# Latent attention of a decoder layer: values in token order, keys in a bank of their own, splits moved, probability turns behind the gate product

## The reference

```python
q = (rms_norm(c_q, q_norm) @ w_uq).reshape(b, s, MLA_HEADS, QK_NOPE + QK_ROPE)      # 384 -> 8 heads x (64 + 32)
kv = (rms_norm(c_kv, kv_norm) @ w_ukv).reshape(b, s, MLA_HEADS, QK_NOPE + V_DIM)    # 256 -> 8 heads x (64 + 64)
k_nope, v = kv[..., :QK_NOPE], kv[..., QK_NOPE:]
# the 32 rotated key features are shared by the heads
logits = q_full @ k_full * (QK_NOPE + QK_ROPE) ** -0.5, causal
y_a = softmax(logits) @ v @ w_br_mla
```

## Time and profile before

| what | value |
|---|---|
| median of 3 runs | 1281.73 us (1281.72 to 1281.84) |
| the profiled execution | 1280.79 us |
| its span | 1279.0 us |
| TensorE busy | 1267.3 us, 5998 matrix instructions |
| Vector, Scalar, GpSimd busy | 669.7, 441.7, 18.8 us |
| granted TensorE clock | 0.998 of full speed |
| latent section on the trace | from 407.0 to 536.9 us |

### The profile page before, as it was taken

The page is one execution under the profiler, slowest core; times in us unless marked ns, Lnnn a source line. Parts: engine busy times, 40 slices in busy tenths (PEclk is TensorE's granted clock), DMA queues, the critical chain, the costliest instruction groups (busy, mean ns, idle before and its releaser), DMA issues.

```text
span 1279.0 us, 16611 instructions
## 1 busy us (share of the span) xinstructions
PE 1267.3 (99%) x5998; PEld 1033.5 (81%) x5998; DVE 669.7 (52%) x984; ACT 441.7 (35%) x763; POOL 18.8 (1%) x36
## 2 busy tenths in 40 slices
PE   9999999999999999999999999999999999999997
PEld 6888888888888777788888888888888888888886
DVE  6744444433336677475665746675644444443323
ACT  6233332322233444343343424423433332232221
POOL 0000000000000000300000000000000000000000
PEclk9999999999999999999999999999999999999999
DMA  6342223333322221622222231222322322233321
GB/s 214 101 111 98 98 98 98 90 91 95 103 92 71 64 70 66 132 67 83 79 78 92 66 99 51 97 89 95 99 96 98 98 98 98 98 90 92 93 88 66
DMA packets 36003, 118.38 MB, mean 93 GB/s; under 512 B 4680, under 2 KB 4680, under 8 KB 35968
## 3 DMA queue, kind: packets, MB, share of 16 engines
q1 hardware_dynamic: 34416, 114.83, 27.8%
q0 software_dynamic: 1264, 3.06, 1.5%
q10 hardware_dynamic: 288, 0.03, 0.0%
HBM read 115.36 MB, written 2.55 MB: 92 GB/s over the span
## 4 chain that ended last, share of the span: by engine, by line
PE 94%; DVE 2%; DMA 1%; issue 1%; ACT 1%; SPq 0%; DVEq 0%; ACTq 0%
PE bank L542 36%; PE bank L376 17%; PE bank L378 17%; PE bank L377 17%; PE bank L725 1%; PE bank L751 1%; PE bank L645 1%; PE bank L672 1%; DVE mla_stats L1451 1%; DMA x<-in_x_t 1%; PE bank L661 1%; PE bank L769 1%; PE bank L765 1%; DMA const<-in_tables 0%; ACT w_hi L358 0%
## 5 line engine op out<-in xcount | busy, mean ns | idle before, releaser
L363 DVE TENSOR_TENSOR w_lo<-raw,w_hi 128x1024 fp32r<-128x1024 f32 (+2 forms) x221 | 258.8, 1171 | 227.6 <-ACT w_hi L358 225.4
L358 ACT ACTIVATE w_hi<-raw 128x1024 fp32r<-128x1024 f32 (+2 forms) x221 | 224.3, 1015 | 433.3 <-PE bank L542 228.3
L542 PE MATMUL bank<-act_hi,w_hi 128*128 128x512 f32 x704 | 218.5, 392 | 0.3 <-DVE w_lo L363 0.3
L542 PE MATMUL bank<-act_hi,w_lo 128*128 128x512 f32 x704 | 217.0, 389 | 0.0
L542 PE MATMUL bank<-act_lo,w_hi 128*128 128x512 f32 x704 | 216.9, 389 | 0.0
L376 PE MATMUL bank<-act_hi,w_hi 128*128 128x512 f32 x528 | 210.7, 399 | 2.0 <-DVE w_lo L363 1.2
L378 PE MATMUL bank<-act_hi,w_lo 128*128 128x512 f32 x528 | 206.2, 390 | 0.0
L377 PE MATMUL bank<-act_lo,w_hi 128*128 128x512 f32 x528 | 205.9, 390 | 0.0
L542 PEld LDWEIGHTS bank<-act_hi,w_hi 128*128 128x128 f32 x704 | 132.2, 188 | 29.6 <-DVE w_lo L363 1.0
L542 PEld LDWEIGHTS bank<-act_hi,w_lo 128*128 128x128 f32 x704 | 132.2, 188 | 27.5
L542 PEld LDWEIGHTS bank<-act_lo,w_hi 128*128 128x128 f32 x704 | 132.2, 188 | 27.4
(11 more groups left out here) (177 smaller groups left out, 1049.3 us busy)
## 6 DMA issues: line engine op xcount, KB each, us to landing
raw<-in_ffn_up SPq DMA_DIRECT2D x87, 512.0 KB, 3.3
raw<-in_w_dil SPq DMA_DIRECT2D x40, 512.0 KB, 3.3
raw<-in_ffn_down SPq DMA_DIRECT2D x32, 448.0 KB, 3.3
raw<-in_ffn_down SPq DMA_DIRECT2D x16, 512.0 KB, 3.5
raw<-in_w_mla_gates SPq DMA_DIRECT2D x8, 512.0 KB, 3.3
raw<-in_w_branches SPq DMA_DIRECT2D x8, 512.0 KB, 3.3
raw<-in_w_out SPq DMA_DIRECT2D x8, 512.0 KB, 3.2
raw<-in_w_latent SPq DMA_DIRECT2D x6, 512.0 KB, 3.3
```

Source lines behind the costliest of these rows:

```text
L358: nc.scalar.activation(w_hi[:, s % SPLIT, 0:tiles * P], raw[:, s % RAW, 0:tiles * P], ACT.Copy).then_inc(hi_ready, 1)
L363: nc.vector.tensor_tensor(w_lo[:, s % SPLIT, 0:tiles * P], raw[:, s % RAW, 0:tiles * P], w_hi[:, s % SPLIT, 0:tiles * P].bitcast(F32), ALU ...
L542: last = nc.tensor.matmul(out, w[:, s % SPLIT, tile * P:(tile + 1) * P], moving[:, row, :], start=row == 0 and w is w_hi and moving is act_hi,
```

## The change

Values: one new group of products (`values`) at the head of the section computes the values of all 8 heads with tokens as rows, from a new piece of weights (`w_values`, 8 tiles): for each block of 128 tokens and each of two latent tiles, three instructions in which the latent tile is the held operand and 512 columns of weights are streamed. Banks 5, 6, 2 and 3 take the four blocks; Scalar copies them to `mla_v` with the norm as scale. `turn_values` and `mla_vt` are gone.

Keys: computed once for a pair of heads (64 + 64 rows of output, 6 instructions) into bank 7, ahead of the queries of the even head. Queries are in bank 0, gates in bank 1. Odd heads load three tiles, even heads five.

Turns: all three parts of the probabilities are turned behind the gate product (in head 7 behind the second dilated product), in banks 5, 6 and 0; the third waits until the next head's query has been read from bank 0.

Weighted values of a pair stand behind the scores of the next even head; those of the last pair stay at the end.

Splits: in head 7 the second dilated piece is rounded ahead of the exponentials and split ahead of the normalization. In the first feed-forward turn the fifth piece is rounded ahead of the first Silu, and split ahead of the wait for it.

The loop of three turns is straight code now on all engines.

```diff
-            load(sp, s, 0, w_lora_up[0], LORA_TILES)
-            load(sp, s + 1, 0, w_mla_gates[0], TILES)
-            with sp.Fori(0, PAIRS - 1) as i:
...
+            load(sp, PIECES["mla"], 0, w_values, TILES)
+            for h in range(MLA_HEADS):
+                at, tiles = (h % 2) * LORA_TILES * P, lora_tiles(h)
+                load(sp, lora_piece(h), 0, w_lora_up[h // 2, :, at:at + tiles * P], tiles)
+                load(sp, lora_piece(h) + 1, 0, w_mla_gates[h], TILES)
```

TensorE:

```diff
+            def values():
+                s = PIECES["mla"]
+                pe.wait_ge(lo_ready, s + 1)
+                pe.wait_ge(chunk_taken, CHUNKS["latent"] + 4)
+                for b, out in enumerate((5, 6, 2, 3)):
+                    block_of = slice(b * P, (b + 1) * P)
+                    for k in range(KKV):
+                        hi, lo = (w[:, s % SPLIT, k * SEQ:(k + 1) * SEQ] for w in (w_hi, w_lo))
+                        latent, rest = (part[:, KQ + k, block_of] for part in (lat_hi, lat_lo))
+                        nc.tensor.matmul(bank[out][:, :], latent, hi, start=k == 0, stop=False)
+                        nc.tensor.matmul(bank[out][:, :], latent, lo, start=False, stop=False)
+                        last = nc.tensor.matmul(bank[out][:, :], rest, hi, start=False, stop=k == KKV - 1)
...
-            def lora(s, d, h, i):
+            def lora(h):
+                s = lora_piece(h)
+                pe.wait_ge(lo_ready, s + 1)
+                if h % 2 == 0:
+                    if h == 0:
+                        pe.wait_ge(mean_ready, 2)
+                    elif h > 2:
+                        pe.wait_ge(mixed_taken, h // 2 - 1)
+                    multiply(s, range(KQ, LORA_TILES), bank[7][:, :], lambda k: lat_hi[:, KQ + k, :],
+                             lambda k: lat_lo[:, KQ + k, :]).then_inc(inner_done, 1)
+                c = query_chunk(h)
+                free_chunk(pe, c)
+                if h > 1:
+                    pe.wait_ge(turned_taken, 3 * (h - 1))
+                multiply(s, range(KQ), bank[c % 2][:, :], lambda k: lat_hi[:, k, :],
+                         lambda k: lat_lo[:, k, :]).then_inc(piece_done, 1)
...
+            def turn_probs(h, part):
+                pe.wait_ge(mla_scaled, 4 * h + 4)
+                if h:
+                    pe.wait_ge(turned_taken, unit - 2)
+                if part == 2:
+                    pe.wait_ge(chunk_taken, (query_chunk(h + 1) if h < MLA_HEADS - 1 else CHUNKS["dil"]) + 1)
...
+            def attention(h):
+                score(h)
+                if h and h % 2 == 0:
+                    attend(h - 1)
                 if h < MLA_HEADS - 1:
-                    lora(s, d, h + 1, i)
+                    lora(h + 1)
                     c = gate_chunk(h)
-                    project(s + 1, d, c + 6 * i, bank[c % 2][:, :], turn_early)
+                    project(lora_piece(h + 1) + 1, 0, c, bank[c % 2][:, :])
                 else:
                     c = CHUNKS["dil"]
+                    pe.wait_ge(turned_taken, 3 * h)
                     project(PIECES["dil"], 0, c, bank[c % 2][:, :])
-                    project(PIECES["dil"] + 1, 0, c + 1, bank[(c + 1) % 2][:, :], turn_early)
-                turn_probs(h, i, 2)
-                if h % 2:
-                    attend(h, i)
+                    project(PIECES["dil"] + 1, 0, c + 1, bank[(c + 1) % 2][:, :])
+                for part in range(3):
+                    turn_probs(h, part)
+                if h == MLA_HEADS - 1:
+                    attend(h)
```

Scalar and Vector, one head each, and the first feed-forward turn:

```diff
+            def attention(h):
+                if h == MLA_HEADS - 1:
+                    split_hi(act, PIECES["dil"] + 1, 0, TILES)
+                exponentials(h)
+                if h < MLA_HEADS - 2:
+                    split_hi(act, lora_piece(h + 2), 0, lora_tiles(h))
+                elif h == MLA_HEADS - 2:
+                    split_hi(act, PIECES["dil"], 0, TILES)
+                else:
+                    split_hi(act, PIECES["dil"] + 2, 0, TILES)
+                take_probs(h)
+                if h < MLA_HEADS - 2:
+                    split_hi(act, lora_piece(h + 2) + 1, 0, TILES)
+                if h < MLA_HEADS - 1:
+                    gate_tanh(gate_chunk(h), h + 1)
+            split_hi(act, lora_piece(0) + 1, 0, TILES)
+            take_values()
+            split_hi(act, lora_piece(1), 0, lora_tiles(1))
+            split_hi(act, lora_piece(1) + 1, 0, TILES)
+            gate_tanh(gate_chunk(-1), 0)
...
+            def attention(h):
+                maxima(h)
+                if h == MLA_HEADS - 1:
+                    split_lo(dve, PIECES["dil"] + 1, 0, TILES)
+                    normalize(h)
+                    split_lo(dve, PIECES["dil"] + 2, 0, TILES)
+                    take_projection(dil_q[:, 0, :], 0, PIECES["dil"], 0, CHUNKS["dil"] % 2)
+                else:
+                    if h % 2:
+                        take_keys(h // 2 + 1)
+                    elif h:
+                        take_mixed(h // 2 - 1, h // 2, bank[7][:, :])
+                    normalize(h)
+                    take_query(h + 1)
+                    if h < MLA_HEADS - 2:
+                        split_lo(dve, lora_piece(h + 2), 0, lora_tiles(h))
+                    else:
+                        split_lo(dve, PIECES["dil"], 0, TILES)
+                    gate_take(lora_piece(h + 1) + 2, gate_chunk(h) % 2, h + 1)
+                    if h < MLA_HEADS - 2:
+                        split_lo(dve, lora_piece(h + 2) + 1, 0, TILES)
...
-                    else:
+                    elif not (first and f == 0):
                         split_hi(act, s + 2, 4 * i, TILES)
                     split_hi(act, s + 3, 4 * i, DOWN_PARTS[1][1] - DOWN_PARTS[1][0] if last and j else TILES)
+                    if first and f == 0 and j == 0:
+                        split_hi(act, s + 4, 0, TILES)
```

More of the change, by code:

```diff
@@ L1049, in _ @@
[L1049 to L1057 removed]
+                    unit = 3 * h + part
@@ L1447, in maxima @@
-            def maxima(h, i):
-                dve.wait_ge(mla_scores, h + 2 * i + 1)
+                c = query_chunk(h)
+                source, out = bank[c % 2], mla_q[:, h % 2, :]
+                dve.wait_ge(piece_done, lora_piece(h) + 1)
+                nc.vector.tensor_copy(out[0:QK_NOPE, :], source[0:QK_NOPE, :])
+                nc.vector.tensor_tensor(out[low, :], source[low, :], rope[low, :], ALU.mult)
+                if h:
+                    dve.wait_ge(head_ready, h)
+                nc.vector.tensor_tensor(rotated[low, :], source[high, :], rope[high, :], ALU.mult).then_inc(chunk_taken, 1)
@@ new lines, in take_query, with take_keys @@
+                dve.wait_ge(chunk_taken, c + 1)
+                nc.vector.tensor_tensor(out[low, :], out[low, :], rotated[low, :], ALU.add).then_inc(head_ready, 1)
+            def take_keys(p):
+                source = bank[7]
+                dve.wait_ge(inner_done, p + 1)
+                nc.vector.tensor_tensor(mla_k[0:QK_NOPE, 0, :], source[0:QK_NOPE, :], rstd_kv[0:QK_NOPE, :], ALU.mult)
+                nc.vector.tensor_tensor(mla_k[0:QK_NOPE, 1, :], source[QK_NOPE:P, :], rstd_kv[QK_NOPE:P, :], ALU.mult)\
+                  .then_inc(keys_taken, 1)
@@ L1780 @@
     up_q = given["w_uq"][0].reshape(Q_LORA, MLA_HEADS, QK_DIM)
-    up_kv = _tiles(given["w_ukv"][0])
+    up_kv = given["w_ukv"][0].reshape(KV_LORA, MLA_HEADS, QK_NOPE + V_DIM)
+    put("w_values", up_kv[:, :, QK_NOPE:].reshape(KKV, P, MLA_HEADS * V_DIM).transpose(1, 0, 2).reshape(P, TILES * P))
     rows = []
-    for h in range(MLA_HEADS):
-        query = np.concatenate([up_q[:, h, :QK_NOPE], _swapped(up_q[:, h, QK_NOPE:])], axis=1)
-        rows.append(np.concatenate([_tiles(query)[0], up_kv[h]], axis=1))
+    for pair in range(MLA_HEADS // 2):
+        first, second = (_tiles(np.concatenate([up_q[:, h, :QK_NOPE], _swapped(up_q[:, h, QK_NOPE:])], axis=1))[0]
+                         for h in (2 * pair, 2 * pair + 1))
+        keys = _tiles(up_kv[:, 2 * pair:2 * pair + 2, :QK_NOPE].reshape(KV_LORA, 2 * QK_NOPE))[0]
+        rows.append(np.concatenate([first, keys, second], axis=1))
     put("w_lora_up", np.stack(rows))
```

220 lines of the change are left out of this document (74 added, 146 removed).

## The result

The changed kernel takes 1272.91 (median of 4 runs, 1272.35 to 1273.30), the one before, beside it, 1281.78 (4 runs, 1281.72 to 1283.47). The ratio is 0.9927, with a 95% interval of 0.9910 to 0.9944: 8.9 us faster, between 7.2 and 11.5. Forecast: 1274.4 in 1272.4 to 1277.4.

The account below looks back on a forecast made before the run. TensorE, busy for 99% of the span, was taken to bound the kernel. Gains of 8.2, less 0.5 and 0.4 lost, make 7.3, taking the median from 1281.73 to 1274.4; range 1272.4 to 1277.4.

Parts of the forecast that it names:

- Products, counted: TensorE's products in the latent section: 48 removed, 48 added, 0.0 net, the side-swapped value group taken at 0.227 each.
- Value transposes, 3.1: Eight groups of four transposes go from the heads, 0.39 each: 3.1 gained, all of it on the path.
- The wait before the gate, 2.2: Gate product waits for a bank Vector still reads; own bank for keys gains 2.2 in heads 0, 1, 3, 5.
- The last head, 1.4: TensorE's 1.56 wait for the second dilated piece ends by splitting it ahead of the normalization: 1.4 gained.
- Turns behind the gate, 1.2: Probability transposes no longer cut the gate group: 0.15 a head, 1.2 gained in eight.
- Weighted values, 0.5 lost: Moved behind next scores: shape change 0.1 in three pairs, last pair's first copy 0.2 late; together 0.5 lost.
- Lateness, 0.4 lost: Scores after head 0 wait for their rotated query: 0.4 lost (bounds 0.2 and 0.8); later heads hold, though barely.
- rival 1: Vector's chain comes late in every second head: 3.6 given back, 1278.0; chance 0.12.
- shape changes: TensorE's switches between kinds of product group; uncertainty of +-0.4 in the forecast's bounds.
- First turn, 0.3: First feed-forward turn: fifth piece rounded ahead of Silu, so TensorE's 0.28 idle before it goes: 0.3 gained.
- Rivals 2 and 3: 2: nothing won, waits only move, 1280 to 1283, chance 0.04; 3: exposed instruction fetches, slower, 1287.6, chance 0.02.

## Why the prediction was right

**In sum.** The result lies in the range, 1.5 under the forecast of 1274.4. On the trace the change gave 8.2 where the net sum was 7.3; the other 0.6 lies in the medians, outside every step. The main mechanism, less work and no waits before the gate and in the last head, is shown. But the sum came out better than its terms, and that is in part luck: 1.0 too much for the turns is made up by shorter scores, which are in no term, and by waits a little larger than I had counted.

**Products, counted: right.** 48 for 48, and the value group with its sides swapped runs at the same 0.227.

**Value transposes, 3.1: size right, "all of it on the path" half right.** Put back into the changed kernel they cost 3.4. But in the kernel before they partly filled the waits in front of the gate: doubled there, they are 2.0 longer and cost 0.6. The two terms are not independent, and 3.1 would not have been had by removing the transposes alone; this part of the inference was not tried by itself. They could be added only because the change removes the waits too.

**The wait before the gate, 2.2: right as a sum, wrong as to its only cause.** All of it is gone. But the bank of its own is worth 0.75 in the new order, and 0.76 would have gone by writing out the loop, to which I gave nothing: I looked for its cost at the ends of the loop, and it is in the handovers of the chain through Scalar and Vector to TensorE. The two figures are from different kernels and don't add up to a price each.

**The last head, 1.4: right.** 1.5 alone. Undone within the change it is 1.9, since without the transposes TensorE arrives 0.5 earlier at the same late split.

**Turns behind the gate, 1.2: wrong.** It is some 0.02 a head, 0.2 in all, and 0.04 net when undone. The step that failed is "the six products after them take 1.47 instead of 1.36, and the three last transposes 0.32 instead of 0.29". Both numbers were read correctly, but the group of seven before them is recorded 0.08 too short (0.68, not 0.76): start-to-start across this border of two kinds of instruction is no duration, only the sum over both sides is. Ten transposes take 1.09, not the 1.0 that I had added up in the same way.

**Weighted values, 0.5 lost: wrong in what it leaves out.** The 0.2 in the last pair was read as 0.19, but 0.1 of it was there before; the loss is 0.1. But the new place is no cost: without it the section is 1.8 longer. It spares three waits for a copy and, in even heads, stands between the scores and the turns, where it covers Vector's chain.

**Lateness, 0.4 lost: right.** Head 0 loses 0.23 ahead of the next scores and 0.1 in them, by the rotated query, as the step said. From the second head on nothing is late, so rival 1 did not come. Its mechanism is real, though: the run with the weighted values at the end shows it in three even heads.

**Where the other 0.9 came from.** For the section the steps gave 7.0 net, the trace 7.8. By the table of groups above, transposes (3.1), last head (1.5 without its cut) and waits before the gate (2.35) make 7.0, where the steps had 6.7. The steps for turns, weighted values and lateness had 1.2 - 0.5 - 0.4 = 0.3; the rows give 0.88 for the uncut gate groups, 0.71 lost in the turns with their waits, and 0.67 gained in the scores: 0.84. The scores are the term that I put at nothing, with shape changes only in the bounds (0.4). Ahead of products they take 2.56, ahead of transposes or weighted values 2.66. The run with the transposes put back shows it: 2.65 again in heads 0, 3, 5 and 7. The parts undone one at a time (3.4, 1.9, 0.75 and 0.0) are not shares of the 7.8, since each also changes what stands behind it.

**First turn, 0.3: right** (0.35). Rivals 2 and 3 fell: the waits did not move elsewhere, and no fetch was exposed.

## What to carry to other kernels

On an engine that is busy for 99%, work and waits ahead of the same release are substitutes: before a removed group is credited with its whole duration, look whether a wait follows it within the same head, and credit the sum only if both go. Read pitches only inside a run of instructions of one kind, across a change of kind take the sum of both sides, and look for short waits in the weight loads' rows. A group that is merely moved has a price by what it stood in front of: placed between a consumer's input and the point where that consumer's answer is due, it is cover.

## What the runs showed of the hardware that I had not expected

- Between float32 transposes (0.109 each) and the products that follow, the first product's start is recorded 0.03 after the last transpose's and the next one 0.32 later (457.71 and 458.03 in the run with early turns); together that is 0.35, and 0.109 + 0.227 is 0.34. A refill of 0.1 doesn't fit in.
- Four 64x64 transposes behind the scores cost 0.39, a further four 0.25.
- The same group takes longer or shorter by what follows it, without a wait: three transposes 0.32 ahead of scores and 0.41 ahead of weighted values, scores 2.56 ahead of products and 2.66 ahead of 64x64 transposes or weighted values.
- A handover between engines took up to 0.1 less in straight code than in the loop, 0.23 over the chain of a head.
- The start of the kernel up to the first token sums varies from 20.8 to 22.6 over the thirteen profiled executions; with one of each variant, and edits that mostly lie behind it, I see no relation to the edit.
